# The last 16 tokens of the first output product in plain float32 on four column groups, and finished tiles taken one step sooner

## The reference

```python
    meta = jnp.broadcast_to(meta_tokens.astype(x.dtype)[None], (B, N_META, D_MODEL))
    h = jnp.concatenate([meta, x], axis=1)
    for l in range(DEPTH):
        hn = rms_norm(h, mix_norm_g[l])
        proj = jnp.einsum('bld,dp->blp', hn, w_in[l])
        q, k, v, cx, cb, cc = jnp.split(proj, splits, axis=-1)
        attn = diff_attention_group(q, k, v, lambda_q1[l], ...)
        conv = cb * centred_depthwise_conv(cc * cx, conv_w[l])
        mixed = jnp.concatenate([attn, conv.astype(attn.dtype)], axis=-1)
        h = h + jnp.einsum('blm,md->bld', mixed, w_out[l])
        h = h + expert_choice_ffn(rms_norm(h, ffn_norm_g[l]), w_router[l], w_gate[l], w_up[l], w_down[l])
```

## Time and profile before

| | us |
|---|---|
| median of 3 runs | 2251.95 (2251.33 to 2252.22) |
| profiled execution, its own time | 2247.52 |
| its span | 2245.6 |
| PE busy | 2184.4 (97%) |
| DVE busy | 1676.4 (75%) |
| ACT busy | 1392.2 (62%) |
| first output product, PE's first to last instruction | 223.94 to 287.63 |
| second output product, from PE's first instruction | 1818.95 |
| last output product, PE's end | 2241.4 |

### The profile page before, as it was taken

One profiled execution on the slowest core, in us unless ns is written; L12 is line 12 of the kernel. 1 busy time (PEld: TensorE's weight loads), 2 busy tenths in 40 slices (PEclk: granted clock), 3 DMA queues, 4 the chain that ended last, 5 costly groups with the idle time before them and its releaser, 6 DMA issues. The chain is left out here.

```text
span 2245.6 us, 31402 instructions
## 1 busy us (share of the span) xinstructions
PE 2184.4 (97%) x11300; PEld 1575.4 (70%) x11300; DVE 1676.4 (75%) x2154; ACT 1392.2 (62%) x1805; POOL 341.0 (15%) x158
## 2 busy tenths in 40 slices
PE   8998989999999999999999999999999999999999
PEld 8987775556556555555556555677797787887777
DVE  6455658898898998898988998756655556885664
ACT  5344456777777777777777777754555455675553
POOL 3033130211220212220212200320000000320000
PEclk9999989999999999999999999999999999999999
DMA  6212349999999999999999999522221131131301
GB/s 183 78 58 94 110 171 343 371 383 384 375 378 375 373 382 384 373 381 376 374 383 387 367 382 373 206 81 89 80 71 57 57 136 37 51 134 38 113 1 38
DMA packets 179654, 506.85 MB, mean 226 GB/s; under 512 B 12541, under 2 KB 57373, under 8 KB 179565
## 3 DMA queue, kind: packets, MB, share of 16 engines
q1 hardware_dynamic: 174813, 494.92, 59.2%
q0 software_dynamic: 4752, 10.75, 2.2%
HBM read 492.99 MB, written 10.48 MB: 224 GB/s over the span
## 5 line engine op out<-in xcount | busy, mean ns | idle before, releaser
L2010 DVE TENSOR_TENSOR pieces_low<-pieces,pieces_high 128x2048 fp32r<-128x2048 f32 x383 | 873.3, 2289 | 110.5 <-ACT pieces_high L1958 105.7
L1958 ACT ACTIVATE pieces_high<-pieces 128x2048 fp32r<-128x2048 f32 x381 | 727.1, 1916 | 238.9 <-PE ps L1882 238.8
L1882 PE MATMUL ps<-pieces_high,ex_x 128*66 128x512 f32 x2080 | 575.9, 394 | 1.9 <-DVE ex_x L2044 1.5
L1882 PEld LDWEIGHTS ps<-pieces_high,ex_x 128*66 128x66 f32 x2080 | 279.9, 137 | 195.9 <-issue 6.9
L1882 PE MATMUL ps<-pieces_low,ex_x 128*66 128x512 f32 x1040 | 324.1, 393 | 0.0
L1882 PE MATMUL ps<-pieces_high,ex_h 128*66 128x512 f32 x992 | 277.4, 394 | 0.0
L483 DVE TENSOR_TENSOR in_w<-ring,in_w 128x256 fp32r<-128x256 f32 (+3 forms) x284 | 135.2, 483 | 161.6 <-ACT in_w L470 159.6
L2321 PE MATMUL ps<-hn_split,in_w 128*128 128x512 f32 (+1 forms) x888 | 227.3, 406 | 5.8 <-DVE hn_split L483 3.2
L1882 PEld LDWEIGHTS ps<-pieces_low,ex_x 128*66 128x66 f32 x1040 | 141.9, 136 | 97.7 <-issue 0.8
L470 ACT ACTIVATE in_w<-ring 128x256 fp32r<-128x256 f32 (+3 forms) x284 | 118.4, 419 | 131.9 <-PE ps L2321 58.6
L1882 PEld LDWEIGHTS ps<-pieces_high,ex_h 128*66 128x66 f32 x992 | 133.7, 136 | 90.7 <-DVE pieces_low L2010 3.2
(11 more groups left out here) (477 smaller groups left out, 2754.7 us busy)
## 6 DMA issues: line engine op xcount, KB each, us to landing
pieces<-in_w_gate SPq DMA_DIRECT2D x128, 1024.0 KB, 7.3
pieces<-in_w_up SPq DMA_DIRECT2D x128, 1024.0 KB, 7.5
pieces<-in_w_down SPq DMA_DIRECT2D x128, 1024.0 KB, 8.8
ring<-in_a_w_in SPq DMA_DIRECT2D x24, 1024.0 KB, 5.1
ring<-in_w_in SPq DMA_DIRECT2D x8, 1024.0 KB, 5.0
ring<-in_b_w_in SPq DMA_DIRECT2D x4, 2048.0 KB, 7.8
ring<-in_b_w_out SPq DMA_DIRECT2D x2, 3072.0 KB, 14.0
ring<-in_w_in SPq DMA_DIRECT2D x8, 512.0 KB, 3.5
```

Source lines behind the costliest of these rows:

```text
L1882: ins = pe.matmul(ps[0:CAP, banks + c, :], parts[a][:, k0 + k, :], w[b][:, k, c * 512:(c + 1) * 512], start=start and k == 0 and a == b == ...
L1958: nc.scalar.activation(m.high[:, n % NSPLIT, :], m.pieces[:, n % NPIECE, :], ACT.Copy).then_inc(high_done, 1)
L2010: nc.vector.tensor_tensor(m.low_part[:, n % NSPLIT, :], m.pieces[:, n % NPIECE, :], m.high[:, n % NSPLIT, :].bitcast(F32), ALU.subtract).t ...
```

## The change

Three things are changed. First, `out1` no longer has the tile of 16 tokens: it gets `TILES1[:tail]`, four tiles, and 6 banks in the order 0, 1, 2, 3, 5, 6. Bank 4 is left for the last 16 tokens, which a new function computes in plain float32, without a split: `tail_products(c)` multiplies, for each of the 8 inner pieces, the 16 tokens with four times 128 columns of the unsplit weight block, each on 32 columns of the array of its own (PSUM partitions 0, 32, 64 and 96). It runs on PE after step 7 for the left and after step 11 for the right columns; `take_tail(c)` on DVE adds the four pieces to the residual rows in rounds 10 and 14. Second, as `tail_products(0)` reads the first weight block itself, that block is free for the next transfer only when it is done (`tail_done`). Third, all three output products get `early=True`, so that finished tiles are taken one round sooner.

```diff
--- before.py
+++ after.py
@@ -757,11 +757,13 @@
     ready[AH].append((s["scored"], 2 * nu))
     ready[0] = [(s["mixed_taken"], nt)]
     bank_waits = {i: [(s["exped"], 2 * nu)] for i in range(4)}
-    bank_waits.update({i: [(s["pt_ready"], nu)] for i in (4,)})
     bank_waits.update({i: [(s["mixed_taken"], nt)] for i in (5, 6)})
     own = m.stage_sems[others:]
-    out = out_gemm(m, "out1", mixed, tok, TILES1, out_slots, ready, [4, 5, 6, 0, 1, 2, 3, 7], banks=7,
-                   bank_waits=bank_waits)
+    out = out_gemm(m, "out1", mixed, tok, TILES1[:tail], out_slots, ready, [4, 5, 6, 0, 1, 2, 3, 7], banks=6,
+                   bank_order=[0, 1, 2, 3, 5, 6], bank_waits=bank_waits)
+    tail_done, tail_taken = m.sem("out1_tail_done"), m.sem("out1_tail_taken")
+    m.block_free[out.first] = (m.stage, tail_done, 1)
+    tail_out = lambda c, g: ps[32 * g:32 * g + TILES1[tail][1], 4, c * P:(c + 1) * P]
     out_on_tensor, out_on_scalar, out_on_vector = beside
     o_bank = lambda t: 5 + t % 3
     pair = lambda i: slice(2 * i, 2 * i + 2)
@@ -906,13 +908,27 @@
                     ins = pe.transpose(ps[:, o_bank(t), h * P:(h + 1) * P], o[:, t, h, :], m.ident)
                 ins.then_inc(s["o_turned"], 1)
 
+            def tail_products(c):
+
+                t0, n = TILES1[tail]
+                pe.wait_ge(*((tail_taken, 1) if c else (s["pt_ready"], nu)))
+                w = m.block_view(out.first + c)
+                for k in range(KD):
+                    for g_ in range(4):
+                        ins = pe.matmul(tail_out(c, g_), mixed[:, k, t0:t0 + n], w[:, k, g_ * P:(g_ + 1) * P],
+                                        start=(k == 0), stop=(k == KD - 1))
+                ins.then_inc(tail_done, 1)
+
             out.products(pe, stop=1)
             for t in range(3):
                 turn_o(t)
             out.products(pe, start=1, stop=2)
             for t in range(3, nt):
                 turn_o(t)
-            out.products(pe, out_on_tensor(pe), start=2)
+            work = out_on_tensor(pe)
+            work.setdefault(7, []).append(lambda: tail_products(0))
+            work.setdefault(11, []).append(lambda: tail_products(1))
+            out.products(pe, work, start=2)
 
         @block.scalar
         def _(act):
@@ -1126,7 +1142,18 @@
             take_o(range(3))
             out.lows(dve, 2)
             take_o(range(3, nt))
-            out.split("dve", dve, out_on_vector(dve), start=3)
+
+            def take_tail(c):
+                dve.wait_ge(tail_done, c + 1)
+                for g_ in range(4):
+                    to = tok[0:TILES1[tail][1], tail, c * 512 + g_ * P:c * 512 + (g_ + 1) * P]
+                    ins = nc.vector.tensor_tensor(to, tail_out(c, g_), to, ALU.add)
+                ins.then_inc(tail_taken, 1)
+
+            work = out_on_vector(dve)
+            work.setdefault(10, []).append(lambda: take_tail(0))
+            work.setdefault(14, []).append(lambda: take_tail(1))
+            out.split("dve", dve, work, start=3)
 
         @block.gpsimd
         def _(pool):
@@ -1193,7 +1220,7 @@
 
     more = {"order": order} if order else {}
     return SplitGemm(m, name, [dict(kind="tokens", act=mixed, tiles=tiles, engine="dve", take=take(c), ready=ready or {},
-                                    **more) for c in range(2)], slots, **banks)
+                                    early=True, **more) for c in range(2)], slots, **banks)
 
 
 def out_stage(m, name, mixed, x, tiles, slots, ahead=2, tail=None, banks=8, beside=(None, None, None), head=None,
```

## The result

The changed kernel takes 2238.57 us, the median of seven runs; one of them was disturbed (3618.54 us at a mean clock of 0.556), and the other six go from 2234.86 to 2242.13 with a median of 2238.19. The kernel before, run beside it, takes 2251.33 (2248.85 to 2252.22). The ratio is 0.9946, with a 95% interval of 0.9935 to 0.9958: 12.2 us faster, between 9.5 and 14.6. Forecast were 9.8 us and 2242.1, with a range from 2240.2 to 2246.6.

A forecast was written before the change was run, and what follows sets the result against it. PE, busy 97% of the span, was taken as the bound. The first output product's 8.29 us and the second's 1.58 made 9.9, taken as 9.8: 2251.95 - 9.8 = 2242.1 us, range 2240.2 to 2246.6.

The forecast's parts named there:

- The small tile: First output product: without the 16-row tile each step is 0.78 us shorter, 0.78 at the start and 10.92 over steps 2 to 15.
- The plain groups: First output product: the 32 plain matmuls on four column groups cost 2.08 us a half, 4.16 for both.
- The drain: Plain groups: draining TensorE at each of four tiling changes makes the sum about 0.6 us worse; worse packing had chance 0.11.
- The 3.07 times: Plain groups: at this packing speedup both cost 5.8 us, 1.6 worse than the sum; worse packing had chance 0.11.
- Step 3: First output product: its split must wait for all takes of the attention result, so PE newly waits 0.52 us.
- The wait in step 8: First output product: PE's 1.27 us wait for DVE's take goes, through the plain group ahead and the earlier takes.
- The second product: Second output product: with takes one round sooner, its whole loss of 1.58 us goes, a wait of 1.29 plus the restart.
- The two transfers: Next stage's weights: the first block waits for the plain group until 254.0, lands at 262, hidden with 18 us to spare.
- The clock in step 1: Rival: the clock falls again after step 0, half clock in steps 1 and 2 gives back 1.6 us: 2243.7, chance 0.15.
- All stages behind are in a chain: Stages behind the first output product: a start 8.3 us sooner should reach the end whole.
- a loss behind the product: Rival: if the experts' first transfers, not the router, set their start, 3 to 5 us are lost: 2246, chance 0.08.
- The runs lie 4.4 us above the profiled execution: Whole kernel: the runs were assumed to stay 4.4 us above the profiled execution, itself forecast at 2237.7 us.

The follow-up runs named there:

- e4: The changed kernel with only the 512 tokens split that the first output product still uses, instead of 528: 2237.81 us, ratio 0.9944.
- e3: The changed kernel with all 32 plain matmuls of a half on one column group, one accumulation after the other: 2250.96 us, ratio 1.0002.
- e1: The kernel before with only the takes of all three output products one round sooner: 2243.4 us, ratio 0.9967.
- e2: The changed kernel with the takes at their old place, so only the small tile moved: 2241.25 us, ratio 0.9961.
- e11: The kernel before with one idle matmul on PE behind the first output product: 2246.17 us in one execution.
- e12: e4 with two idle matmuls ahead of step 0, three ahead of the experts' first transposes and one behind them: 2246.53 us, ratio 0.9987.
- e9: The kernel before with two idle matmuls on PE behind the first output product: 2248.53 us, ratio 0.9996.
- e10: The changed kernel with two idle matmuls on PE behind the first output product: 2242.05 us, ratio 0.9959.

## Why the prediction was right in its mechanism and wrong in its number

**The small tile: right, with a term mis-sized.** "The tile costs 0.78 us a step" took the step that is left from the last output product, at 0.2266 us per matmul. In its own place it is 0.2337, as it was before, so a step is 2.80 us and the tile cost 0.70. Over the start and 14 steps that is 15 x 0.08 = 1.2 us less than the 11.70 in the sum, and the largest error in the product's terms. e4 brings the distance to 0.230 by the shorter rows of `out_a`, about half of the difference to the last product. Where the rest comes from stays open.

**The plain groups: right.** A group lasts 1.87 us to the start of what follows. With the 0.16 that the step ahead of it is longer and some 0.05 behind it, it costs 2.08, which is what was taken. e3 shows that it is the overlap of four groups that makes them cheap. The drain of the Trainium skill, TensorEngine Tiling, "Key Properties", was priced at 0.6 us more. The 3.07 times of the Trainium skill, TensorE: Matmul & The Clock Gate, "Measured speedup vs the span model", were priced at 1.6 us more. Neither showed in these traces, and the rows of the attention were the better guide.

**The waits: right, one of them undersized.** Step 3 starts 3.24 us behind step 2, exactly as forecast, of which 0.44 is lost (the row's idle time of 0.21 leaves out the restart). The wait in step 8 is gone; of the two reasons given one is enough (e1, e2). It was worth more than its 1.27: 1.55 in e1, since the restart of PE goes with it, which the sum counted in the second product and not here. The second product gave 1.57 where 1.58 was forecast, and the last product nothing. The two transfers moved to 258.76 in the profile and had landed by 277.48, 8 us before their first reader at 285.48. In the first product this makes 8.29 - 1.18 + 0.28 + 0.08 = 7.47, which is what was measured; together with the second 9.04 against 9.87.

**The clock in step 1: a rival that is real.** It happened in 4 of the 14 executions profiled (e2, e4, e11 and e12) at the 1.6 us that were given, and in none of the three of the changed kernel. The form was another than the rival's: not a second fall behind that of step 0, but the one fall in step 1 instead of step 0.

**What failed is the way from the stage to the runs.** Two sentences of the sum carried it. One: "All stages behind are in a chain, so a start 8.3 us sooner should reach the end whole." It reached the end, and more came with it. I had looked for a loss behind the product and priced it (2246), and never for a gain: time at half clock behind the product was put at nothing without a reason, though one view of the stretches from 304 to 314 us would have shown 10 us at 0.50 of the clock in a stage that PE bounds. That is worth 2.6 us. The stages of the two products and the router together are 11.7, and the runs say 12.2 (9.5 to 14.6).

Two: "The runs lie 4.4 us above the profiled execution, and I assume that they stay there." They did not: 0.8 for the changed kernel. Three profiled executions of before give 2247.2 on average against medians of 2249.7 to 2251.3, three of the changed kernel 2236.9 against 2238.6. The distance of a single profiled execution to the median is not a property of the kernel, and the forecast of the median hung on it.

The mean granted clock of each timed execution, which is on record to 0.001, ties the two together. It is 0.9911 on average in 38 runs of the kernel before, the lowest of all kernels measured here, and 0.9927 in six of the changed kernel. Within a kernel a run is about 1.44 us longer for each 0.001 less (an estimate of mine: one slope through 101 runs of nine kernels). At equal clock the changed kernel is then 8.9 us (+-1.1) faster than before, e1 3.1 and e4 9.1, where the products alone say 9.0, 3.1 and 9.4; e2 and e3 fit less well, 6.4 and -2.3 (slower) against 7.5 and -1.4. The difference of the clocks, 0.0016, makes 2.3 us more, and the 11.2 lie within the interval of the 12.2. So what the forecast of the median lacked, as far as the record shows it, is that the changed kernel spends less time at half clock. How much less is known poorly: six runs leave the mean clock open by +-0.0015, some 2 us, and a part of the miss may be luck. The profiled executions of before had 0.992, 0.993 and 0.992, more than their kernel's mean, which goes with their being quick; that three of three were so can be chance.

**What stays open.** How the beginning of the router stage decides over the clock in it: the stage times of e9, e11 and e10 rest on one profiled execution each, and e2, e3 and e4 had a fall there (of 3.4, 10.2 and 10.2 us) while e1 and e12 had none. The fall was there in some executions and gone in others of kernels whose router stage begins within 1 us of each other behind the product; the profiles don't show a rule. How often this fall occurs in the timed executions isn't seen, since their mean clock doesn't say in which stage it fell. Measured by time alone, e10 is 3.5 us above the changed kernel, where 1.0 is its filler and 3.4 the fall, and e9, which should be 2.1 quicker than before, is 0.9 quicker: both agree with a fall that some executions have and others don't.

## What to carry to other kernels

A tile of 16 rows in a split product cost as much as one of 128 here; moved out and laid side by side on four column groups, it cost a quarter of what its matmuls cost one behind the other, and only that made moving it pay. When a change is worth a few parts in a thousand, add it up by stages over several profiled executions of both kernels, compare the mean clocks of the timed ones, and look for stretches at a low clock in the stages that merely move: such a stretch can vanish or appear without an edit there. And take the duration of a matmul from the place that the change leaves it in, not from a like product elsewhere, and count the restart with every wait that goes.

## What the runs showed of the hardware that was not expected

- With PE busy for 4.00 of 4 us, the granted clock was 0.50 in the router stage of the kernel before (306 to 310 us above, about 304 to 314 in all). A busy share of 100% was no sign of the full clock here. The matmuls of 16 columns that run there took 284 ns each on average, and 257 where the clock didn't fall.
- The distance of two fp32r matmuls of 512 columns was 0.2337 us with `out_a` in rows of 528, 0.230 in rows of 512 and 0.2266 in the last product.
- A plain float32 matmul of 128 columns with 16 stationary columns took 0.222 us in a row on one column group and 0.058 (1.87 / 32) on four.
- A fall of the clock in step 0 cost nothing and the same fall in step 1 cost 1.6 us, because DVE's split sets the start of step 1.
